# A hybrid decoder step on one Trainium2 core: the order of the attention's work on TensorE, wider key products, cache pages read earlier, four loop iterations written out

## The chip, the cores and the metric

The kernel runs on one NeuronCore of a Trainium2 chip. The metric is device time in microseconds (us) of one execution. Three runs of the kernel before took 1240.34, 1240.37 and 1240.64 us, with a median of 1240.37. The profiler's picture of one more execution (1240.44 us) gives the rows below.

## The reference

One inference step of a two-layer trunk with D = 1024, for 256 prompt tokens of one sequence and 64 sample tokens (8 sequences of 8). Layer 0 is half-FFN, mLSTM, half-FFN. Then one shared pair of keys and values is projected. Layer 1 is half-FFN, attention with 8 heads of 128, half-FFN, and a final RMSNorm. All is f32. Cut to the attention that the change touches:

```
# prompt: causal inside 256 tokens;  sample: 256 cached keys in 2 pages of 128, and 8 new ones
k_past = cache_k[page_table]          # pages of (128 keys, 8 heads, 128)
s = q @ k.T * 128**-0.5 - slope[head] * distance      # masked where distance < 0
out = softmax(s) @ v                  # per head, then @ w_out_b and x = x + out
```

With 256 keys and a block of 256 every query attends to all earlier keys.

## The kernel before

The 256 + 64 = 320 tokens are the moving columns of nearly every product; the weights are stationary, in tiles of 128 x 128. Weights come by DMA in units of 1 MB (or 0.7 MB) into a ring `raw` of four slots. ScalarE writes the upper part of each unit (`w_hi`), VectorE the lower part (`w_lo`), and TensorE adds three products in PSUM (`passes`, L556 to L558). A `pair_unit` is 16 such triples (two output chunks, 48 matmuls); an `out_chunk` of an FFN is 22 triples (66 matmuls). An FFN is 22 pair units and 8 output chunks. Most of them run in hardware loops: nine iterations of two pair units, three iterations of two output chunks. The third FFN (`f == 2`) is the one ahead of the attention; between them stand the four units of the query projection.

Each engine has an instruction list of its own, written out by hand, and semaphores order the lists. A change of one list does not move the others except through these waits. For the attention the lists are as follows.

**TensorE.** For prompt head h, `prompt_scores(h)` multiplies queries by keys (L954, L955). `prompt_turn(h)` transposes the probabilities with three transposes (L965). `prompt_outputs(h)` multiplies them by the values (L975, L976). For the sample tokens, 4 heads of 32 rows are packed into one PSUM bank. A product for one head then uses a 32-column strip of the array, and four strips work side by side. `new_scores` (L984) takes the new keys, and `cache_scores(b)` (L1001, L1007) the cached keys of sequence b. `turn_new_probs` and `turn_page_probs` (L1018, L1024) transpose, `new_outputs` (L1037) takes the new values and `cache_outputs(b)` (L1059) the cached ones. A *cached unit* c is the keys of sequence c for c < 8 and the values of sequence c - 8 otherwise. The order before puts these units into six visits, with prompt work between: units 0 and 1; 2 to 4; 5 to 7; 8 to 11; 12 to 14; 15. `turn_early_outputs` and `turn_late_outputs` (L1070, L1081) transpose the sample outputs. Then the output projection `w_ob` starts; its first product waits for the lower parts of head 0 and of the first late sample rows.

**Cache pages.** Cached units 0 to 3 and 9 to 12 use slots of the ring `raw`; the other eight use `rooms`, buffers that are otherwise idle at that time. In the ring the two pages of keys are one operand of 256 moving columns per head (L1007, 8 products a unit). In a room each page is multiplied by itself, 128 columns (L1001, 16 products a unit).

**SP (SyncE)** issues all weight and cache loads in one list. `page_of` (L493) reads a page number into a register with `value_load` and directly after it the DMA is issued (L504 in the ring, L509 in rooms). Each load waits for its slot (`slot_free`). Units 7 and up wait for the last unit of the query projection.

**ScalarE and VectorE.** ScalarE has `prompt_exp`, `prompt_copy` (transposed probabilities out of PSUM, L1545), `prompt_hi` (L1549), `sample_exp`, `sample_rows` and `late_hi` (L1568). VectorE has `prompt_bias` with the maxima (L2122, L2127), `prompt_probs` (L2134), `prompt_lo` (L2140), `sample_bias` (L2147), `spread_probs` (L2157, L2161) and `late_lo` (L2177). The prompt probabilities `pp` have two buffers, so the bias of head h waits for the transpose of head h - 2. All transposes of prompt probabilities use bank 6, one after the other. GpSimd clears `q_spread`, `p_spread` and `p_new` ahead of the attention.

Of the kernel before, what the change touches and what calls it, by code (L numbers as in the profile page):

```python
# [19 lines left out]
KT = D // 128  # L20
# [49 lines left out]
def trunk_program(nc, w_in, w_out, w_a, w_oa, w_kv, w_q, w_ob, w_gate, xp_in, con_in, row_in,  # L70
# [6 lines left out]
    with ctx:  # L77
# [30 lines left out]
        pp = work[:, 0:768].rearrange("p (s k) -> p s k", s=2)  # L108
        pt = work[:, 768:1536].rearrange("p (s k) -> p s k", s=2)
# [14 lines left out]
        with ExitStack() as ov:  # L124
# [35 lines left out]
            with ExitStack() as own:  # L160
# [9 lines left out]
                st = sb("st", [128, 2, 6], f32, own)  # L170
                sst = sb("sst", [128, 3, 4], f32, own)

        rooms = [[page_k[:, 0:1024], page_k[:, 1024:2048]], [keys_room[:, 0:1024], keys_room[:, 1024:2048]],
                      [row_room[:, 0:1024], norm_room[:, 0:1024]]]
        for at in (PAIR, 3 * PAIR):
            rooms.append([split_room[:, at:at + 1024], split_room[:, at + 1024:at + 2048]])
# [220 lines left out]
        def prompt_score_bank(h):  # L397

            return bank[{1: 6, H - 1: 1}.get(h, 5)]
# [31 lines left out]
        def _(sp):  # L431
# [60 lines left out]
            sp.wait_ge(s_pg, 16)  # L492
            def page_of(c, j):  # L493

                at = NPG * (c % NB) + j
                page = sp.value_load(pages[0:1, at:at + 1], min_val=0, max_val=kc_in.shape[0] - 1)
                return (kc_in if c < NB else vc_in)[bass.ds(page, 1), :, :].rearrange("a p c -> p (a c)")
# [55 lines left out]
        def _(pe):  # L553
# [103 lines left out]
            def ffn(f, h_wait, between, behind=None, values=0):  # L657
# [289 lines left out]

            def prompt_scores(h):
                if 2 <= h < H - 1:
                    pe.wait_ge(pr_b, h if h > 2 else 1)  # L950
                elif h == H - 1:
                    pe.wait_ge(sm_tc, 9)
# [5 lines left out]
            def prompt_turn(h):  # L958
# [5 lines left out]
                for i in range(3):  # L964
                    mm = pe.transpose(bank[6][:, i * 128:i * 128 + 128],  # L965
                                      pp[:, h % 2, i * 128:i * 128 + 128], ident)
# [20 lines left out]
            def cache_scores(b, groups=(0, 1)):  # L987
# [7 lines left out]
                for g in groups:  # L995
                    out = bank[2 * g + b // 4]
                    if early is not None:
# [6 lines left out]
                    else:  # L1004
                        keys = raw[:, raw_of_cache(b) % RAW, :].rearrange("p (j h k) -> p j h k", j=NPG, h=H)
# [7 lines left out]
            def turn_new_probs(i):  # L1013
# [3 lines left out]
                w = SLOT * (r % 2) + SLOT  # L1017
                pe.transpose(bank[r][0:w, 256:384], ss[:, r, PAST + SLOT - w:PAST + SLOT], ident)  # L1018
# [12 lines left out]
            def new_outputs(q):  # L1031

                outs = outs_of(q)
                pe.wait_ge(sm_tc, 6 * q + 6)
                for h in range(H):
# [48 lines left out]
            pe.wait_ge(x_ready, 4 * KT)  # L1084
            prompt_scores(0)
            prompt_scores(1)
            new_scores(0)
# [7 lines left out]
            cache_scores(0, (1,))  # L1095

            def cache_unit(c):

                if c < NB:
                    cache_scores(c)  # L1100
                else:
                    cache_outputs(c - NB)

            cache_unit(1)

            prompt_scores(2)
            prompt_turn(0)
            cache_unit(2)
            cache_unit(3)
            pe.wait_ge(qa_sp, 4)  # L1110
            cache_unit(4)

            prompt_outputs(0)
            prompt_scores(3)
            prompt_turn(1)
            cache_unit(5)
            cache_unit(6)
            cache_unit(7)

            turn_new_probs(0)  # L1120
            turn_page_probs(0)
            prompt_scores(4)
# [1339 lines left out]
```

## Time and profile before

| what | value |
|---|---|
| median of three runs | 1240.37 us |
| the profiled execution | 1240.44 us |
| its span in the trace | 1238.6 us |
| TensorE busy (matmuls; weight loads) | 1233.2 us; 1210.4 us |
| VectorE, ScalarE, GpSimd busy | 726.1; 582.7; 81.1 us |
| attention stage, 936.80 to 969.08 | 32.28 us |
| moved by DMA | 200.39 MB |

Busy time of an engine is the union of its records. A matmul's record lasts longer than the distance to the next one (309 ns each for the 320-column products, which follow one another about every 147 ns), because matmuls are pipelined and their ends are modelled. So a TensorE that is shown busy all the time can still pause; pauses are read from the distance between starts. PE is TensorE's matmuls, PEld its weight loads, DVE is VectorE, ACT is ScalarE, POOL is GpSimd. The largest groups of the page are all L556 to L558.

### The profile page before, as it was taken

What the parts mean: (1) busy time and instruction counts of PE and PEld (TensorE: products, weight loads), DVE (VectorE), ACT (ScalarE), POOL (GpSimd) and SP (SyncE); (2) the same over time, 40 slices, a digit from 0 to 9 for tenths busy, and PEclk for the clock granted to TensorE, in tenths of its full rate; (3) what the DMA queues carried; (4) which work ended last, traced back from release to release, by engine and by line L of the source; (5) the groups of instructions that cost most, each with busy time, mean ns of one, the idle gap of its engine ahead of it and who ended that gap; (6) DMA issues with size and microseconds to landing.
All of it is one profiled execution on the core that took longest, in us unless ns stands there. A gap on an engine that the chain in (4) does not pass through costs nothing.

```text
span 1238.6 us, 22056 instructions
## 1 busy us (share of the span) xinstructions
PE 1233.2 (100%) x8875; PEld 1210.4 (98%) x8875; DVE 726.1 (59%) x1127; ACT 582.7 (47%) x936; POOL 81.1 (7%) x99
## 2 busy tenths in 40 slices
PE   9999999999999999999999999999999999999998
PEld 9999999989999999999998999999998999999998
DVE  7656554575777656555564565655467585565443
ACT  6534333464556445443345554534344474544343
POOL 0000000100332000000000000000020110000010
PEclk9999999999999999999999999999999999999999
DMA  8344334543354443334543734334478734433341
GB/s 341 137 161 144 112 132 155 205 147 131 127 164 147 157 166 137 134 121 140 187 166 137 262 136 151 143 105 153 163 277 317 287 139 142 163 135 127 125 156 43
DMA packets 34778, 200.39 MB, mean 162 GB/s; under 512 B 4050, under 2 KB 4186, under 8 KB 19490
## 3 DMA queue, kind: packets, MB, share of 16 engines
q1 hardware_dynamic: 32706, 192.24, 44.0%
q0 software_dynamic: 2016, 7.39, 1.9%
q8 instruction: 38, 0.62, 0.2%
q14 instruction: 18, 0.15, 0.0%
HBM read 193.03 MB, written 6.57 MB: 161 GB/s over the span
## 4 chain that ended last, share of the span: by engine, by line
PE 99%; DMA 0%; SPq 0%; DVE 0%; ACT 0%; issue 0%; DVEq 0%
PE bank L556 30%; PE bank L558 30%; PE bank L557 29%; PE bank L714 1%; PE bank L713 1%; PE bank L712 1%; PE bank L716 1%; PE bank L715 1%; PE bank L1059 1%; DMA xp<-xp_in 0%; PE bank L867 0%; PE bank L822 0%; PE bank L975 0%; PE bank L1001 0%; PE bank L1007 0%; PE bank L955 0%
## 5 line engine op out<-in xcount | busy, mean ns | idle before, releaser
L556 PE MATMUL bank<-h_hi,w_hi 128*128 128x320 f32 x1792 | 555.6, 310 | 0.5 <-DVE h_lo L1682 0.5
L558 PE MATMUL bank<-h_hi,w_lo 128*128 128x320 f32 x1792 | 553.8, 309 | 0.0
L557 PE MATMUL bank<-h_lo,w_hi 128*128 128x320 f32 x1792 | 553.7, 309 | 0.0
L1222 ACT ACTIVATE w_hi<-raw 128x1024 fp32r<-128x1024 f32 (+1 forms) x364 | 331.7, 958 | 440.7 <-PE bank L558 421.7
L1668 DVE TENSOR_TENSOR w_lo<-raw,w_hi 128x1024 fp32r<-128x1024 f32 (+1 forms) x364 | 388.5, 1108 | 133.1 <-ACT w_hi L1222 133.0
L556 PEld LDWEIGHTS bank<-h_hi,w_hi 128*128 128x128 f32 x1792 | 336.3, 188 | 2.6 <-issue 1.4
L557 PEld LDWEIGHTS bank<-h_lo,w_hi 128*128 128x128 f32 x1792 | 336.4, 188 | 0.1
L558 PEld LDWEIGHTS bank<-h_hi,w_lo 128*128 128x128 f32 x1792 | 336.3, 188 | 0.0
L557 PE MATMUL bank<-f_lo,w_hi 128*128 128x320 f32 x704 | 216.5, 308 | 0.0
L558 PE MATMUL bank<-f_hi,w_lo 128*128 128x320 f32 x704 | 216.5, 308 | 0.0
L556 PE MATMUL bank<-f_hi,w_hi 128*128 128x320 f32 x704 | 216.5, 308 | 0.0
L1711 DVE TENSOR_TENSOR work<-bank,rms 128x320 f32<-128x320 f32 x88 | 43.2, 491 | 152.0 <-PE bank L558 151.5
L558 PEld LDWEIGHTS bank<-f_hi,w_lo 128*128 128x128 f32 x704 | 131.9, 187 | 0.0
L556 PEld LDWEIGHTS bank<-f_hi,w_hi 128*128 128x128 f32 x704 | 131.9, 187 | 0.0
L557 PEld LDWEIGHTS bank<-f_lo,w_hi 128*128 128x128 f32 x704 | 131.9, 187 | 0.0
L1272 ACT ACTIVATE f_hi<-work 128x320 f32 (+1 forms) x88 | 41.5, 472 | 124.0 <-DVE work L1719 124.0
L1726 DVE TENSOR_TENSOR f_lo<-work,f_hi 128x320 f32 (+1 forms) x88 | 43.3, 492 | 64.5 <-ACT f_hi L1272 64.5
L2281 POOL TENSOR_TENSOR norm_room<-norm_room 128x320 f32<-128x320 f32 x41 | 43.8, 1068 | 264.9 <-ACT norm_room L1244 263.7
L1731 DVE SCALAR_TENSOR_TENSOR xp<-bank,xp 128x320 f32<-128x320 f32 x31 | 15.3, 493 | 67.3 <-PE bank L558 67.3
L2278 POOL COPY norm_room<-norm_room 128x320 f32<-128x320 f32 x6 | 5.0, 836 | 723.1 <-ACT norm_room L1244 723.1
L1682 DVE SCALAR_TENSOR_TENSOR h_lo<-xp,h_hi 128x320 fp32r<-128x320 f32 x56 | 44.8, 833 | 3.4 <-ACT h_hi L1247 3.4
L1719 DVE TENSOR_TENSOR work<-work 128x320 f32<-128x320 f32 x88 | 42.8, 486 | 4.8 <-ACT work L1268 4.8
(263 smaller groups left out, 763.0 us busy)
## 6 DMA issues: line engine op xcount, KB each, us to landing
raw<-w_in SPq DMA_DIRECT2D x86, 1024.0 KB, 4.8
raw<-w_out SPq DMA_DIRECT2D x64, 704.0 KB, 4.0
raw<-w_a SPq DMA_DIRECT2D x12, 1024.0 KB, 4.7
raw<-w_kv SPq DMA_DIRECT2D x8, 1024.0 KB, 4.7
raw<-w_oa SPq DMA_DIRECT2D x4, 1024.0 KB, 6.0
raw<-w_q SPq DMA_DIRECT2D x4, 1024.0 KB, 4.7
raw<-w_ob SPq DMA_DIRECT2D x4, 1024.0 KB, 11.8
raw<-kc_in SPq DMA_DIRECT2D x8, 512.0 KB, 4.5
```

Source lines behind the costliest of these rows:

```text
L556: pe.matmul(out, wh, mh, start=first, stop=False)
L557: pe.matmul(out, wh, ml, start=False, stop=False)
L558: return pe.matmul(out, wl, mh, start=False, stop=last)
L1222: sc.activation(w_hi[:, n_at % 2, part * w:part * w + w], raw[:, raw_of(n_at) % RAW, part * w:part * w + w], ACT.Copy).then_inc(hi_done, 1)
L1272: sc.activation(dst, up[:, k_at % 2, :], ACT.Copy).then_inc(hid_hi, 1)
L1668: ins = ve.tensor_tensor(w_lo[:, n_at % 2, c], raw[:, raw_of(n_at) % RAW, c], w_hi[:, n_at % 2, c].bitcast(f32), ALU.subtract)
L1682: ve.scalar_tensor_tensor(out=h_lo[:, m, :], in0=x[:, m, :], scalar=par[:, P_G + KT * norm + m:P_G + KT * norm + m + 1], in1=h_hi[:, m, :] ...
L1711: ve.tensor_tensor(gate[:, k_at % 2, :], bank[b][:, 0:T], rms[:, :], ALU.mult).then_inc(gate_ready, 1)
L1719: ve.tensor_tensor(up[:, k_at % 2, :], up[:, k_at % 2, :], act[:, k_at % 2, :], ALU.mult).then_inc(hid_ready, 1)
L1726: ve.tensor_tensor(lo, up[:, k_at % 2, :], hi.bitcast(f32), ALU.subtract).then_inc(hid_lo, 1)
L1731: ve.scalar_tensor_tensor(out=x[:, m, :], in0=bank[4 + m % 2][:, 0:T], scalar=0.5, in1=x[:, m, :], op0=ALU.mult, op1=ALU.add).then_inc(x_r ...
L2281: gp.tensor_tensor(sqsum[:, :], sqsum[:, :], sq[:, m % 2, :], ALU.add).then_inc(sum_done, 1)
```

## The change

It does five things. (1) TensorE's list in the attention is in a new order: prompt scores of heads 0, 1 and 2 first, then cached units in four visits (0 to 6; 7 to 11; 12 to 14; 15). ScalarE's and VectorE's lists follow. Prompt scores of heads 2 and 4 go to bank 4, and `pp` and `st` have three buffers. (2) Rooms that are contiguous are used with 256-column key products as in the ring (cached units 4, 5 and 7; unit 6 lies in two tensors and stays as it was). (3) `turn_new_probs` transposes 128 columns of a widened `ss`, whose tail GpSimd clears. (4) SP reads the page numbers of units 7 to 13 ahead, between earlier loads. (5) In the third FFN the last two iterations of both loops are written out on TensorE.

```
-        pp = work[:, 0:768].rearrange("p (s k) -> p s k", s=2)
+        pp = work[:, 0:1152].rearrange("p (s k) -> p s k", s=3)
-                ss = sb("ss", [128, 4, PAST + SLOT], f32, own)
+                ss = sb("ss", [128, 4, PAST + 128], f32, own)
+        rooms = [[both[:, 0:1024], both[:, 1024:2048], both]
+                 for both in (page_k, keys_room, split_room[:, PAIR:2 * PAIR], split_room[:, 3 * PAIR:4 * PAIR])]
+        rooms.insert(2, [row_room[:, 0:1024], norm_room[:, 0:1024], None])
-            return bank[{1: 6, H - 1: 1}.get(h, 5)]
+            return bank[{1: 6, 2: 4, 4: 4, H - 1: 1}.get(h, 5)]
...
+            def read_pages(units):
+                for c in units:
+                    for j in range(NPG):
+                        at = NPG * (c % NB) + j
+                        page_read[c, j] = sp.value_load(pages[0:1, at:at + 1], min_val=0,
+                                                        max_val=kc_in.shape[0] - 1)
...
             load_room(6, 1)
+            read_pages((7,))
             load_cache(1)
+            read_pages((NB, NB + 1, NB + 2))
             load_cache(2)
+            read_pages((NB + 3, NB + 4, NB + 5))
             load_cache(3)
...
-                with pe.Fori(0, (FK - 4) // 2) as i:
+                looped = (FK - 4) // 2 - (2 if f == 2 else 0)
+                with pe.Fori(0, looped) as i:
-                pair_unit(u + FK - 1, p + FK - 1, u + FK - 1, p + FK - 1)
+                units(u, p, 3 + 2 * looped, FK)
...
-                with pe.Fori(0, (KT - 2) // 2) as i:
+                out_looped = (KT - 2) // 2 - (2 if f == 2 else 0)
+                with pe.Fori(0, out_looped) as i:
                     for j in (2, 3):
                         out_chunk(i * 2 + j, j, False)
+                for m in range(2 + 2 * out_looped, KT):
+                    out_chunk(m, m, False)
...
-                w = SLOT * (r % 2) + SLOT
-                pe.transpose(bank[r][0:w, 256:384], ss[:, r, PAST + SLOT - w:PAST + SLOT], ident)
+                at = PAST - SLOT * (r % 2)
+                pe.transpose(bank[r][:, 256:384], ss[:, r, at:at + 128], ident)
...
+            gp.memset(ss[:, :, PAST + SLOT:PAST + 128], 0.0).then_inc(spread_set, 1)
```

TensorE's list after the change, from the first prompt scores to the output projection (waits left out; S = prompt_scores, T = prompt_turn, O = prompt_outputs, n and p = turn_new_probs and turn_page_probs, N = new_outputs, bracketed numbers = cached units):

```
before: S0 S1 new_scores [0 1] S2 T0 [2 3 4] O0 S3 T1 [5 6 7] n0 p0 S4 T2 O1 n1 n2 S5 p1 p2 O2 T3
        N0 [8 9 10 11] n3 p3 O3 T4 S6 S7 T5 O4 N1 [12 13 14] T6 O5 early [15] T7 O6 late0 O7 late1
after:  S0 S1 S2 new_scores [0 1 2 3 4 5 6] T0 S3 n0 p0 T1 O0 S4 n1 T2 S5 p1 O1 [7] N0 [8 9 10 11]
        T3 O2 n2 S6 p2 T4 n3 O3 early p3 S7 T5 O4 N1 [12 13 14] O5 T6 [15] T7 O6 late0 late1 O7
```

## Rows read from the trace of the kernel before

**Rows 1.** The page: the span, and the chain of waits by engine.
```profile
span 1238.6 us, 22056 instructions
...
PE 99%; DMA 0%; SPq 0%; DVE 0%; ACT 0%; issue 0%; DVEq 0%
```

**Rows 2.** Stage table: stretch, length, busy time (records), clock, DMA share, GB/s.
```profile
936.80:969.08 32.28, 32.28 (x618) 26.84 (x617) 24.98 (x85) 16.99 (x59) 0.00 (x0) 1.00 1.00 380
...
970.00:1229.90 259.90, 259.90 (x1774) 259.90 (x1773) 140.93 (x197) 121.23 (x171) 18.28 (x15) 1.00 0.39 136
```

**Rows 3.** TensorE's timeline, entering two visits: start, length to the last end, operation, count.
```profile
937.68 0.60 PE L955 MATMUL bank<-k_all,qa 128*128 128x256 f32 x2
938.20 0.33 PE L984 MATMUL bank<-k_all,qa 128*32 128x32 f32 x16
...
961.38 0.65 PE L1037 MATMUL bank<-v_tok,p_new 128*32 128x128 f32 x16
961.84 1.06 PE L1059 MATMUL bank<-raw,p_spread 128*32 128x128 f32 x32
962.72 1.06 PE L1059 MATMUL bank<-page_k,p_spread 128*32 128x128 f32 x32
```

**Rows 4.** TensorE's timeline, the second visit, and what follows the fifth.
```profile
941.19 0.55 PE L965 MATMUL bank<-con,work 128*128 128x128 f32 x3
941.67 1.93 PE L1007 MATMUL bank<-raw,q_spread 128*32 128x256 f32 x32
943.42 1.06 PE L1001 MATMUL bank<-page_k,q_spread 128*32 128x128 f32 x32
944.41 0.70 PE L975 MATMUL bank<-work,v_tok 128*128 128x256 f32 x2
944.94 0.39 PE L976 MATMUL bank<-work,v_tok 128*128 128x128 f32 x2
...
964.58 0.55 PE L965 MATMUL bank<-con,work 128*128 128x128 f32 x3
964.96 0.60 PE L975 MATMUL bank<-work,v_tok 128*128 128x256 f32 x2
```

**Rows 5.** TensorE's timeline around the narrow transposes of new probabilities.
```profile
948.01 1.06 PE L1001 MATMUL bank<-split_room,q_spread 128*32 128x128 f32 x32
949.00 0.28 PE L1018 MATMUL bank<-con,ss 128*32 128x128 f32 x1
...
950.98 0.38 PE L1018 MATMUL bank<-con,ss 128*32 128x128 f32 x2
951.32 0.49 PE L954 MATMUL bank<-k_all,qa 128*128 128x128 f32 x2
```

**Rows 6.** SP's timeline: page issues of cached units 1 to 3, then unit 7.
```profile
921.65 14.00 SPq L504 DMA_DIRECT2D raw<-kc_in  x6
937.71 1.44 SPq L509 DMA_DIRECT2D split_room<-kc_in  x2
```

**Rows 7.** All engines' timeline at the end of the attention.
```profile
967.52 0.49 ACT L1545 ACTIVATE work<-bank 128x384 f32<-128x384 f32 x1 [0.52 <-PE bank L965]
...
968.02 0.27 PE L1081 MATMUL bank<-con,o_rows 128*128 128x128 f32 x1
...
968.33 0.28 ACT L1568 ACTIVATE h_hi<-bank 128x128 fp32r<-128x128 f32 x1 [0.32 <-PE bank L1081]
...
968.64 0.29 DVE L2177 TENSOR_TENSOR h_lo<-bank,h_hi 128x128 fp32r<-128x128 f32 x1 [0.90 <-ACT h_hi L1568]
...
969.08 0.38 PE L556 MATMUL bank<-h_hi,w_hi 128*128 128x320 f32 x1
```

**Rows 8.** DMA of 936.80 to 969.08, instruction queue: packets, MB, share of 16 engines.
```profile
q8 instruction: 5, 0.08, 1.0%
```

**Rows 9.** DMA issues of 934 to 936 and 942 to 950.5, median us to landing.
```profile
raw<-kc_in SPq DMA_DIRECT2D x2, 512.0 KB, 4.6
...
raw<-vc_in SPq DMA_DIRECT2D x8, 512.0 KB, 7.1
```

More of the change, by code:

```diff
@@ L166, in trunk_program @@
                 p_new = sb("p_new", [128, 4, 128], f32, own)
-                ss = sb("ss", [128, 4, PAST + SLOT], f32, own)
+                ss = sb("ss", [128, 4, PAST + 128], f32, own)
                 o_rows = sb("o_rows", [128, 4, DV], f32, own)
                 page_k = sb("page_k", [128, 2048], f32, own)
-                st = sb("st", [128, 2, 6], f32, own)
+                st = sb("st", [128, 3, 6], f32, own)
                 sst = sb("sst", [128, 3, 4], f32, own)
[L173 to L176, printed above, removed]
+        rooms = [[both[:, 0:1024], both[:, 1024:2048], both]
+                 for both in (page_k, keys_room, split_room[:, PAIR:2 * PAIR], split_room[:, 3 * PAIR:4 * PAIR])]
+        rooms.insert(2, [row_room[:, 0:1024], norm_room[:, 0:1024], None])
         ident, ones = con[:, C_ID:C_ID + 128], ones_r[:, :].bitcast(f32)
@@ L492, in _ @@
             sp.wait_ge(s_pg, 16)
+            page_read = {}
+            def read_pages(units):
[4 more added lines that the diff above has]
+                                                        max_val=kc_in.shape[0] - 1)
             def page_of(c, j):
-                at = NPG * (c % NB) + j
-                page = sp.value_load(pages[0:1, at:at + 1], min_val=0, max_val=kc_in.shape[0] - 1)
-                return (kc_in if c < NB else vc_in)[bass.ds(page, 1), :, :].rearrange("a p c -> p (a c)")
+                if (c, j) not in page_read:
+                    read_pages((c,))
+                return (kc_in if c < NB else vc_in)[bass.ds(page_read[c, j], 1), :, :].rearrange("a p c -> p (a c)")
             def load_cache(c):
@@ L996, in cache_scores @@
                     out = bank[2 * g + b // 4]
-                    if early is not None:
+                    if early is not None and rooms[early][2] is None:
                         for j in range(NPG):
@@ L1004, in cache_scores @@
                     else:
-                        keys = raw[:, raw_of_cache(b) % RAW, :].rearrange("p (j h k) -> p j h k", j=NPG, h=H)
+                        both = raw[:, raw_of_cache(b) % RAW, :] if early is None else rooms[early][2]
+                        keys = both.rearrange("p (j h k) -> p j h k", j=NPG, h=H)
                         for k in range(QB):
@@ L1084, in _, with cache_unit @@
             pe.wait_ge(x_ready, 4 * KT)
+            def cache_unit(c):
+                if c < NB:
+                    cache_scores(c)
+                else:
+                    cache_outputs(c - NB)
             prompt_scores(0)
             prompt_scores(1)
+            prompt_scores(2)
             new_scores(0)
@@ L1095, in _ @@
             cache_scores(0, (1,))
[L1097 to L1106, printed above, removed]
-            prompt_turn(0)
[L1108 to L1113, printed above, removed]
+            for c in range(1, 4):
+                cache_unit(c)
+            pe.wait_ge(qa_sp, 4)
+            for c in range(4, 7):
+                cache_unit(c)
+            prompt_turn(0)
             prompt_scores(3)
[L1115 to L1118, printed above, removed]
             turn_new_probs(0)
             turn_page_probs(0)
+            prompt_turn(1)
+            prompt_outputs(0)
             prompt_scores(4)
+            turn_new_probs(1)
             prompt_turn(2)
-            prompt_outputs(1)
-            turn_new_probs(1)
-            turn_new_probs(2)
             prompt_scores(5)
             turn_page_probs(1)
-            turn_page_probs(2)
-            prompt_outputs(2)
-            prompt_turn(3)
+            prompt_outputs(1)
+            cache_unit(7)
             new_outputs(0)
@@ L2119, in prompt_bias @@
                 ve.wait_ge(pr_s, h + 1)
-                if h >= 2:
-                    ve.wait_ge(pr_t, h - 1)
-                ve.scalar_tensor_tensor(out=pp[:, h % 2, :], in0=con[:, C_ND:C_ND + 384], scalar=SLOPE[h],
+                if h >= 3:
+                    ve.wait_ge(pr_t, h - 2)
+                ve.scalar_tensor_tensor(out=pp[:, h % 3, :], in0=con[:, C_ND:C_ND + 384], scalar=SLOPE[h],
                                         in1=prompt_score_bank(h)[:, 0:384], op0=ALU.mult, op1=ALU.add
```

104 lines of the change are left out of this document (55 added, 49 removed).

## The prediction

> **What bounds the kernel now.** I read the page first, then the stage table, then the timeline of the one stage that the change touches. The page says that TensorE is busy in all of the 1238.6 us and that the chain of waits lies on it for 99% [rows 1]. So time comes off only where TensorE does less, or where the starts of its instructions lie further apart than their columns ask. The stage table puts the attention at 936.80 to 969.08, 32.28 us, 618 matmul records, at the full granted clock (1.00, the 2.4 GHz level); the long stretch behind it, 970 to 1229.9, has the same clock and a full busy share [rows 2]. That busy share hides pauses, since ends are modelled. The timeline shows them: I subtract start from start.
>
> The unit of account is one pass (an f32 product is two passes and two records, a transpose one). A cached unit of 128-column products is 32 records in eight slots of four passes side by side, 961.84 to 962.72: 0.109 us a slot [rows 3]. Two units with 256-wide keys are 32 records from 941.67 to 943.42, less 0.02 of entry (below) 1.73 us in eight slots: 0.216 us [rows 4]. All that is more is pause.
>
> **Where the pauses are.** Entering a visit of cached products (four 32-column tiles side by side) from whole-array work: 937.68 to 938.20 is 0.52 against 2 x 0.216, so 0.09; then 961.38 to 961.84 is 0.46 against 4 x 0.109, so 0.02. Together 0.12 us with the thousandths [rows 3]. Leaving: the unit from 943.42 takes 0.99 against 0.875, so 0.11 before the next product, and that product's two 256-column passes take 0.53 against 0.43, so 0.10 more: 0.22 into a product. Into three transposes: from 962.72 [rows 3] to 964.58 lie two units of 0.875, which leaves the same 0.11 of 1.86, and 964.58 to 964.96 is 0.38 against 0.33: 0.17 in all [rows 4]. Into a narrow transpose (32 columns stationary): 948.01 to 949.00 gives 0.12, and I take 0.13; the two narrow ones at 950.98 take 0.34 against 0.22 before a product begins, and with the product's own second pause that is 0.22 once more [rows 5].
>
> **The change part by part.**
> 1. *Visits.* Before there are six: out of them the exits cost 0.22, 0.22, 0.13, 0.14, 0.17 and 0.17, the narrow pair 0.22, and six entries 6 x 0.12 = 0.72. Sum 1.99 us. After there are four, and what follows them is a transpose (heads 0, 3 and 7) or a product (outputs of head 5): 4 x 0.12 + 3 x 0.17 + 0.22 = 1.21. The transposes of new probabilities now have 128 stationary columns and need no switch. Gain 0.78.
> 2. *The wait of the first prompt transpose.* At 941.19 it starts 0.11 late, held by the first probabilities, and its three passes and the entry behind them show the loads uncovered: 0.48 to 941.67 against 0.33 + 0.09, so 0.06 [rows 4]. After, it stands behind seven cached units, 945.3 instead of 941.2, and the probabilities are ready at about 941. Gain 0.17. What is late next is in 6.
> 3. *256-wide keys in rooms.* Units 4, 5 and 7 go from 16 products to 8. A narrow unit is 8 x 0.109 = 0.875, a wide one 4 x 0.216 = 0.865: gain 0.01 each, 0.03 [rows 3, 4].
> The page TensorEngine Tiling (Array Packing) of the Trainium skill, section Instruction Overhead, speaks of some 60 cycles for each matmul; by it 24 products fewer would give 24 x 25 ns = 0.6 us. The trace disagrees (0.875 against 0.865 us), and the sum goes by the trace.
> 4. *Three prompt scores ahead.* The same products in another place; they need only bank 4, whose last reader is done when x is ready. Price 0. Cover: none needed, TensorE does them anyway.
> 5. *Pages read ahead, on SP.* A page goes out every 1.10 us with its read (two issues in 1.44 us, the last 0.34), the issue alone being 0.34, so a read is at most 0.76 us and six are at most 4.6 [rows 6]. I take 0.57, half of the 1.10 and a little, 3.4 us for six. Read between cached loads 1 and 2 and between 2 and 3, they fall into waits for a free slot: the six issues of loads 1 to 3 take 14.00 us for work of 6 x 1.1, so some 3.7 us of wait stand ahead of each of 2 and 3. Load 3's second page still goes out at 935.3, at the bound 4.6 up to 1 us later, and B below has room for 1.7. Behind it the queue gets shorter: units 7 to 12 go out in about 0.55 instead of 1.10 us a page, so the values and the output weights come earlier than before. Gain on TensorE 0, bounds: 0 (nothing waits for a transfer now) and -0.8 (a late page, below). The extra memset of 384 columns on POOL ends near 920, and its wait on VectorE stands at 933. Price 0.
> 6. *Waits of the new order.* I carried each engine's list along with its durations: copy of transposed probabilities 0.49, upper part 0.28 and lower part 0.29 us for late sample rows [rows 7], 0.1 more for a whole head, and on VectorE, start to next start, bias with maxima 1.11 and probabilities 0.66. The tightest places on TensorE, by how long before need the word comes: transpose 1 behind copy 0, 0.1 us; outputs 2 behind lower part 1, 0.1; outputs 3 and 4, 0.2 each; transpose 7, 0.25; the second new outputs behind the last spread probabilities, 0.3. Behind a waiting instruction here everything on TensorE waits. Bounds: 0 (all covered) and 0.3 us (several missed by 0.05 to 0.1, each with its 0.06 to 0.10 of uncovered load). I take 0.
> 7. *The end.* The first product of the output weights waits for the lower part of the late sample rows. Before: transpose at 968.02, upper part 968.33, lower part 968.64, product 969.08, that is 1.06 us from transpose to product [rows 7]. That chain stays, and in both orders the last outputs (0.65) and the other late transpose (0.11) stand behind this transpose and fit into the 1.06. So TensorE stands some 0.3 us here after as before, and what counts is what lies ahead of 968.02: 0.78 + 0.17 + 0.03 = 0.98 us, and the transpose comes at 967.04. Bounds: 0, and 0.1 gained by short waits ahead of the last outputs that I cannot tell from the rounding.
> 8. *Four loop iterations written out.* The loop bodies are the same products. Branches show no cost: 970 to 1229.9 holds nine and three iterations of these loops, and TensorE and its loads are both busy 259.90 of 259.90 us [rows 2]. What the edit adds is code: 4 x 96 + 4 x 132 = 912 records in straight line. In the attention 1235 records took five instruction loads, one per 247, so it adds 3.7 loads, and each takes 1.0% x 16 x 32.28 / 5 = 1.03 us of a DMA engine [rows 8]. With a load per some 18 us of such stages (247 records, matmuls 0.147 us apart with a weight load each) the load is far ahead. Value 0; bounds -1.03 us (one load uncovered) and 0 (no iteration boundary costs anything that could come back).
> The page Advanced Engine Details and Errata of the Trainium skill, section ISA Cache, says that instructions come in lines of 256; by that rule, the trace agrees (247), and straight code has to be fetched where a loop had not.
>
> **The sum.** Of the profiled execution: 1238.6 - 0.98 = 1237.6 us span; with the 1.84 around it, 1240.44 - 0.98 = 1239.46. It stands 0.07 above the median 1240.37, and from that the same sum gives 1239.4, which I predict.
>
> **The rivals.**
> A. *Instruction supply (the slower side).* The new order packs seven cached units in a row and shifts by 912 records where each load falls. Where 128-column products run, 64 records (with their weight loads) pass in 0.875 us and 247 in 3.4 us, against 1.03 us for a load while the DMA share is 1.00 [rows 2]. One load uncovered gives 1239.4 + 1.03 = 1240.4; from the second on the kernel is slower, 1241.4. It decides when the loads are late by more than 0.98 us in total. For it: more straight code, full rings. Against: five loads in the same stage now, without a pause that the switches do not explain.
> B. *A page is late.* Cached unit 3 is wanted at 941.7 instead of 942.5. It lands at 935.3 + 4.6 = 939.9 [rows 9]; if the four page loads that now follow faster stretch it to the 7.1 us of the value pages [rows 9], it lands at 942.4, 0.7 to 0.8 late: 1240.2.
> C. *The vector and scalar engines are late.* The margins of 6 are missed: 0.3 us, 1239.7.
> D. *The pauses are not those of the switch*, but come with the first product of any group that changes operands; then fewer visits bring nothing and only the removed wait counts: 1240.2. Against: prompt scores followed by prompt scores, and transposes by products, run without a pause.
> E. *A fixed cost per product*, which fewer products save: 24 of them at the 0.02 that the first slot of a visit costs [rows 3] give 0.5 more, 1238.9. Against: the 0.875 and 0.865 of part 3.
>
> **How the numbers follow.** Forecast 0.69, A 0.10 (0.06 of it one load), B 0.05, C 0.08, D 0.04, E 0.04. Within 0.2% (2.5 us; about what can be told from no change) lie all of these but several uncovered loads: same 0.93. Slower by more needs 3.5 us of them, 0.04; faster by more has no term, 0.03. The range 1238.8 to 1240.6 holds the forecast, B to E, and one load of A.
>
> **What would show it.** The first product of the output weights at 968.1. Four entries of 0.09 and none at the transposes of new probabilities. First prompt transpose at 945.3 with no wait for VectorE. Cached unit 3 without a pause. No gap over 0.1 us in the rest of the third FFN, above all where the loops end. I am wrong if TensorE stands for an instruction load or a page, or if exits cost less or more in the new neighbourhood.

## The result, and the profile after

| kernel | median | runs, lowest to highest |
|---|---|---|
| before, same chip | 1240.24 us | 16, 1239.94 to 1240.64 |
| changed | 1243.30 us | 16, 1241.60 to 1244.09 |

The ratio is 1.0021 with a 95% interval of 1.0014 to 1.0028: slower, and outside the range forecast. The medians differ by 3.1 us; the ratio alone would give 2.6, since the runs are split as follows. The changed kernel's runs fall into two groups: six of 1241.6 to 1242.1 us have a granted clock of 1.000, ten of 1243.2 to 1244.1 us one of 0.998 or 0.999. The profiled execution, 1243.27 us, is of the second.

The page of the changed kernel, the lines that answer to [rows 1]: the span is 2.9 us longer and the chain is still TensorE's.
```profile
span 1241.5 us, 21936 instructions
...
PE 99%; DMA 0%; issue 0%; SPq 0%; DVE 0%; ACT 0%; DVEq 0%
```

Its stage table (columns as in [rows 2]): the attention, then a stretch within it.
```profile
936.67:972.42 35.75, 33.27 (x570) 27.61 (x569) 25.04 (x86) 17.88 (x61) 0.00 (x0) 0.95 0.99 398
957.28:960.80 3.52, 3.52 (x37) 2.94 (x29) 0.00 (x0) 0.86 (x2) 0.00 (x0) 0.52 1.03 410
```
The attention is 35.75 us long instead of 32.28, 3.47 more. TensorE, busy throughout before, now has 35.75 - 33.27 = 2.48 us without a record, and for 3.5 us its clock is half (0.52).

Where this lies is in its timeline (start, length to the last end, operation, count, in brackets the idle time ahead and what ended it):
```profile
944.84 0.40 PE L1019 MATMUL bank<-norm_room,q_spread 128*32 128x128 f32 x8
945.17 0.55 PE L983 MATMUL bank<-con,work 128*128 128x128 f32 x3
...
949.93 0.38 PE L994 MATMUL bank<-work,v_tok 128*128 128x128 f32 x2
950.24 1.07 PE L1026 MATMUL bank<-split_room,q_spread 128*32 128x256 f32 x16
951.13 0.62 PE L1058 MATMUL bank<-v_tok,p_new 128*32 128x128 f32 x16
951.57 1.06 PE L1080 MATMUL bank<-split_room,p_spread 128*32 128x128 f32 x32
952.44 1.48 PE L1080 MATMUL bank<-raw,p_spread 128*32 128x128 f32 x44
956.38 2.33 PE L1080 MATMUL bank<-raw,p_spread 128*32 128x128 f32 x52 [2.46 <-issue]
958.64 0.90 PE L983 MATMUL bank<-con,work 128*128 128x128 f32 x3
959.34 1.06 PE L993 MATMUL bank<-work,v_tok 128*128 128x256 f32 x2
960.19 0.64 PE L994 MATMUL bank<-work,v_tok 128*128 128x128 f32 x2
```
TensorE stops in the middle of cached unit 10, between two products of one line that wait for nothing ("issue"). I call such a stop a stand. By starts the gap is 953.65 to 956.38: 2.63 us over the slot of 0.109. From 0.9 to 1.0 us after the restart a slot takes 0.213 us instead of 0.109, until 960.8: the last row but one, the two passes of a 256-column product, takes 0.85 instead of 0.43. This stretch costs some 3.52 x (1 - 0.52) = 1.7 us. So 2.63 + 1.7 were added, and the rest is 3.47 - 4.33 = -0.86: the saving. The medians of the two groups of runs lie 1243.4 - 1241.8 = 1.6 us apart, about the half-clock stretch. So I read the groups as the stand in all runs and the lower clock behind it in ten; only one execution has a trace.

What is missing is the supply of instructions. Rows of four answers of the DMA view: the kernel before from its border (explained below) to 953.1 and from there 0.1 us on, then the changed kernel likewise. q1 carries pages and weights, q8 instructions; the share is that of the time of 16 DMA engines:
```profile
q1 hardware_dynamic: 297, 1.08, 103.4%
...
q8 instruction: 1, 0.02, 69.3%
```
```profile
q1 hardware_dynamic: 718, 2.61, 102.0%
...
q8 instruction: 1, 0.02, 67.2%
```
The first row of each covers 950.54 to 953.10 in the kernel before and 947.41 to 953.75 in the changed one, and no instruction packet is among its packets; the second covers 953.10 to 953.20 and 953.75 to 953.85, and the packet starts there. A load brings 256 instructions (one packet of 0.02 MB; the changed kernel has 41 loads for its 10571 instructions, the kernel before 38 for 9750). I counted TensorE's instructions in the program, weight load and matmul one each. All the stands below lie at a number that is 215 or 216 modulo 256, here 8408: I call such a place a border. In the kernel before, the load needed at the border of 956.5 us starts 2.6 us behind the border ahead of it; here it starts 6.4 us behind (953.79, border 947.41), when TensorE has already started its last product ahead of the stand (953.65). In every kernel with a stand TensorE goes on 2.2 to 2.6 us after such a late load's start, though its packet takes 0.9 to 1.1: here 956.38 - 953.79 = 2.59.

The other rows of the forecast came out. Entries of 0.09 and 0.02, four of them. An exit into transposes of 0.11 and then 0.06: the two slots from 944.84 end at 945.06, and the first transpose starts at 945.17. No pause at the transposes of new probabilities. The first prompt transpose at 945.17 without a wait. SP's issues, with the landing times of the value pages:
```profile
937.00 0.85 SPq L518 DMA_DIRECT2D split_room<-kc_in  x2
938.03 0.85 SPq L518 DMA_DIRECT2D split_room<-vc_in  x2
940.25 5.63 SPq L513 DMA_DIRECT2D raw<-vc_in  x8
```
```profile
raw<-vc_in SPq DMA_DIRECT2D x8, 512.0 KB, 9.4
```
Two issues take 0.85 where they took 1.44 [rows 6]; the values land after 9.4 instead of 7.1 us [rows 9], and nothing waits for them here.

### The profile page after: what moved, and what is told of

It is laid out like the page before. It is cut to its first block, busy times and chain, and to the rows that moved or that the text cites. A ratio compares the mean times of both kernels' runs of the same rounds, so it can differ in the third digit from the quotient of the medians.

```text
span 1241.5 us, 21936 instructions
## 1 busy us (share of the span) xinstructions
PE 1233.8 (99%) x8827; PEld 1210.7 (98%) x8827; DVE 726.2 (58%) x1127; ACT 583.3 (47%) x936; POOL 81.4 (7%) x100
## 4 chain that ended last, share of the span: by engine, by line
PE 99%; DMA 0%; issue 0%; SPq 0%; DVE 0%; ACT 0%; DVEq 0%
PE bank L568 30%; PE bank L570 29%; PE bank L569 29%; PE bank L730 1%; PE bank L729 1%; PE bank L728 1%; PE bank L1080 1%; PE bank L732 1%; PE bank L731 1%; PE bank L1026 0%; DMA xp<-xp_in 0%; PE bank L883 0%; PE bank L838 0%; PE bank L993 0%; PE bank L973 0%; PE bank L983 0%
```

## The experiments

Each job ran the kernel before on the same chip: 1240.57 us in the first job, 1240.28 in the second, 1240.39 in the third, 1240.24 in the fourth. "Order" is the new order with three-deep buffers.

### First job: the parts one by one

`e1_reads_on_demand`, the page reads back at their loads (both of a unit together):
```
-            read_pages((7,))
-            read_pages((NB, NB + 1, NB + 2))
-            read_pages((NB + 3, NB + 4, NB + 5))
```


> The changed kernel, but SP reads each page number right before its DMA as before the change. In the changed kernel TensorE stood from 953.65 to 956.38 us in the middle of a cached unit, with no semaphore there, and an instruction load started at that moment. Theory Q (queue): the pages issued 0.52 us apart instead of 1.10 us fill the DMA rings (value pages landed after 9.4 to 13.6 us instead of 7.1), and the instruction load that TensorE needs waits behind them; then here the load comes in time, no stand, 1239.4 us. Theory P (place): the new order and the written-out iterations put the border between two instruction loads into a run that TensorE works off too fast for any load; then the stand of 2 to 3 us stays, 1242 to 1243.5 us.

1242.06 us (1240.73 to 1243.81), ratio 1.0014 [1.0005, 1.0023]. The stand is there, 2.9 us at the same instruction 8408. The reads ahead are not its cause. The clock of this profiled execution stays full behind it.

`e2_loops_kept`, the loops as they were:
```
-                looped = (FK - 4) // 2 - (2 if f == 2 else 0)
+                looped = (FK - 4) // 2
-                out_looped = (KT - 2) // 2 - (2 if f == 2 else 0)
+                out_looped = (KT - 2) // 2
```


> The changed kernel with all loop iterations of the third FFN in the loops again; page reads stay ahead. All borders between instruction loads move by 912 records (156 within a load of 256). Theory Q: the rings are as full as in the changed kernel, but the distance between borders around the visit of units 8 to 11 grows from 6.2 to 8.2 us (943.98 to 952.22 by the records of the changed kernel), so the stand shrinks to 0 to 1 us: 1239.4 to 1240.5 us. Theory P: the dense run still holds a border, so a stand of 2 to 3 us stays, elsewhere: 1242 to 1243.5 us.

1242.35 us (1241.18 to 1243.93), ratio 1.0013 [1.0004, 1.0022]. The stand at 8408 is gone and another is there, 2.2 us at instruction 7896, border again, with half clock behind it; and TensorE waits 0.7 us for the page of unit 11 (0.9 by starts). Taking the written-out iterations away moves the loss and does not remove it.

`e3_before_written_out`, the kernel before with part 8 alone, and `e4_before_reads_ahead`, with part 5 alone:

> The kernel before with only the four loop iterations written out. Theory Q: page loads go out as slowly as before, instruction loads are some 3 us late and need 2.6 us more to be usable, and the borders lie 7.7, 7.3, 5.1 and 5.4 us apart, so at most a stand of 0.6 us near 959.4: 1240.2 to 1241. Theory P: writing out is what puts a border into a dense run, so a stand of 2 to 3 us with the half clock behind it: 1242 to 1244 us. If nothing of both: 1240.2.

> The kernel before with only the page numbers read ahead on SP. Theory Q: the rings fill as in the changed kernel, an instruction load is 5 to 6 us late plus 2.6, and the borders lie 5.7 to 6.8 us apart, so TensorE stands 1 to 3 us: 1241.5 to 1244 us. Theory P: borders are where they were, no stand, 1240.2 us.

e3: 1240.79 us, ratio 1.0002 [0.9993, 1.0011], a stand of 0.5 us at a border (8919). e4: 1240.29 us, 0.9997 [0.9988, 1.0006], attention 32.28 us, no stand, though its value pages land after 9.6 us as in the changed kernel. Neither part alone costs what was lost: for e3 theory Q's time holds, for e4 theory P's.

### Second job: place and traffic

`e5_order_and_width`: both edits of e1 and e2 together, so that only the order and the wide keys are left.

> The changed kernel with its page reads back beside their loads and its loops kept: only the order of the visits and the width of the keys are left of the change. TensorE's program is the one of the run with the loops kept, so its borders of 256 instructions (at 216 modulo 256) stand at the same places. Theory P (place: a load of 256 instructions comes too late where TensorE gets through the 256 before it too fast): the stand in the last value visit, at about 964.5 us, stays, 1.5 to 2.5 us, and the time is 1241.2 to 1243 us. Theory O (the order itself costs, by late pages or waits of vector and scalar work, and the instructions are a side effect): a time of 1241 to 1243 us too, but with a wait for a semaphore of over 0.5 us in the attention. If neither: no stand, 1239.4 us, and the written-out iterations would be the whole loss.

1242.83 us (1241.34 to 1245.60), ratio 1.0021 [1.0012, 1.0030]. A stand of 1.93 us at 7896 and, as the theory O had it, a wait for a page:
```profile
PE bank L1077 <- issue: 1.8, 1, 1.8
PE bank L1077 <- DMA raw<-vc_in: 1.2, 1, 1.2
```
So the order, with the wide keys, brings a loss of this size without the other parts, in two kinds: where no instruction stand delays TensorE ahead of unit 11, that unit's page is late. The order also moves which products lie between two borders, so this run doesn't tell the two apart.

`f1_one_pair_iteration` (the changed kernel) and `f2_before_one_pair_iteration` (the kernel before) move the borders by writing out one iteration of the pair loop and none of the other:
```
-                looped = (FK - 4) // 2 - (2 if f == 2 else 0)
+                looped = (FK - 4) // 2 - (1 if f == 2 else 0)
-                out_looped = (KT - 2) // 2 - (2 if f == 2 else 0)
+                out_looped = (KT - 2) // 2 - (0 if f == 2 else 0)
```


> The changed kernel with one loop iteration of the fused pairs written out instead of two and two: TensorE's attention begins at instruction 7050 instead of 7772, so its borders fall 78, 334, 590, 846 and 1102 products and weight loads behind its start instead of 124, 380, 636, 892 and 1148. Nothing else differs. Theory P: the stretches between borders then take 5.6, 8.1, 8.1 and 4.6 us without a stand (7.3, 6.6, 8.1, 5.6 in the changed kernel), so no stand in units 8 to 11, at most one of under 1 us at the last border (about 966 us): 1239.3 to 1240.5 us. Theory R (the instruction load is held up by the full DMA rings, wherever the border is): a stand of 2 us or more somewhere between 948 and 958 us, 1242 to 1243.5 us. Theory S (the spare length of the program, more loads in all, is what costs): between, in proportion to 39 loads instead of 41, about 1241.

> The kernel before with one loop iteration of the fused pairs written out, nothing else. Its attention then begins at instruction 7050 and its borders fall 78, 334, 590, 846 and 1102 behind that; between the third and the fourth TensorE needs only 3.5 us (5.5 us in the kernel before, whose shortest this is beside 6). Theory P: a stand of 1.5 to 2 us at about 957.5 us (846 instructions into the attention), with or without a stretch at half clock behind it of up to 1.7 us: 1241.7 to 1243.9 us, in the order of before. Theory R: the pages are issued 1.1 us apart as in the kernel before, the rings hold 2 MB at most, so no stand: 1240.3 us.

f1: 1242.17 us (1241.42 to 1242.82), ratio 1.0015 [1.0006, 1.0024], stands of 1.73 and 0.86 us and one of 0.3 us at 945.13, all at borders. Theory P had none at the place of the 1.73; it fails as stated, since the load there starts 7.4 us behind its border. Theory R's time fits (1242 to 1243.5), its stand of 2 us or more does not.

f2: 1244.58 us (1244.18 to 1245.93), ratio 1.0035 [1.0023, 1.0047], the slowest of all, with the order, the widths and the page issues of the kernel before. Its stage table row and the rows at the first stand:
```profile
936.88:974.34 37.46, 34.62 (x619) 28.38 (x617) 24.98 (x85) 17.11 (x59) 0.00 (x0) 0.95 0.98 378
```
```profile
955.00 2.78 PE L1063 MATMUL bank<-raw,p_spread 128*32 128x128 f32 x90
959.80 0.42 PE L1063 MATMUL bank<-raw,p_spread 128*32 128x128 f32 x6 [2.01 <-issue]
...
960.51 1.06 PE L979 MATMUL bank<-work,v_tok 128*128 128x256 f32 x2
```
The stand (2.17 us, at 957.51) comes where P put it, a second of 1.0 us follows at 968.1, and the last row shows the half clock (0.86 us for the two passes of a 256-column product). The time is 0.7 us above P's upper bound; P had one stand. One written-out iteration, in a stretch of 320-column products that itself takes no longer (the attention begins at 936.88 instead of 936.80), costs 4.3 us some 130 us later: the last branch of its loop is at 807.4 us, one iteration takes 14.1. This shows that the kernel before is free of stands only by where its borders fall.

`f3_small_value_pages` leaves out 15/16 of the cached values from the second value unit on, in the changed kernel:
```
+                n = 1024 if c <= NB else 64
-                    sp.dma_start(raw[:, r % RAW, j * 1024:j * 1024 + 1024], page_of(c, j)
+                    sp.dma_start(raw[:, r % RAW, j * 1024:j * 1024 + n], page_of(c, j)[:, 0:n]
```


> The changed kernel with 64 instead of 1024 columns of each cached value page read from the second value unit on (so 15/16 of those values are left out, and what the room held is used in their place); all instructions and waits of TensorE are as in the changed kernel. Theory R: with the rings nearly empty between 941 and 953 us the instruction load starts within 3 us of TensorE's crossing of the border at 947.4 us, the stand at 953.6 us is gone, 1239.3 to 1239.8 us. Theory P in its strict form (the load takes the same time whatever the rings hold): the stand of 2.6 us stays at the same instruction, 1241.6 to 1243.3 us.

1239.26 us (1239.01 to 1239.71), ratio 0.9992 [0.9983, 1.0001]. Of the stand 0.17 us is left.
```profile
936.77:968.44 31.67, 31.65 (x570) 26.29 (x569) 25.04 (x86) 17.95 (x61) 0.00 (x0) 1.00 0.68 239
```
TensorE's program is the same to the instruction, so traffic has a part in it: the load starts at 951.41, 2.4 us earlier. But the load still starts 3.9 us behind its border, with these rows from the border (947.51) to 951.38, and from there 0.1 us on:
```profile
q1 hardware_dynamic: 432, 0.10, 11.3%
...
q8 instruction: 1, 0.02, 70.4%
```
What the expectations call rings, the DMA queues by q1's share, is all but empty (11.3%) while it has not started, so traffic is not all that holds it.

### Third job: controls

`g1_before_small_value_pages`: the same cut in the kernel before.

> The kernel before with 64 instead of 1024 columns of each cached value page read from the second value unit on (15/16 of those values left out). A control for the changed kernel with the same cut, which took 1239.26 us. Theory G (that run shows the 0.98 us that the visits and the turns save, with the stand gone): there is no stand in the kernel before that could go, so 1240.2 us, attention 32.2 to 32.3 us long, and the two differ by 0.9 to 1.0 us. Theory H (emptier rings by themselves give the time back): 1239.3 us here too.

1240.31 us (1240.13 to 1240.68), ratio 0.9999 [0.9990, 1.0008].
```profile
936.74:969.02 32.28, 32.28 (x619) 26.84 (x617) 24.97 (x85) 16.99 (x59) 0.00 (x0) 1.00 0.63 219
```
Theory G holds. Against f3 the medians differ by 1.05 us. In the attention 0.60 us of it is seen, 0.77 without f3's 0.17 of stand, where the sum had 0.98; in the profiled executions 0.35 us more lies behind TensorE's last product, in no term of the sum.

This run says something of the loads too. With the pages full, those that follow the borders of 950.54 and 956.5 us start 2.6 and 3.0 us behind them (953.12 and 959.52). Here they start at 950.27, 0.3 us ahead, and at 956.80, 0.3 us behind, in the same program of TensorE. So the traffic holds a load back by some 3 us.

`g2_one_pair_small_pages`: the cut in f2.

> The kernel before with one pair iteration written out (1244.6 us, stands of 2.17 and 1.01 us and half clock behind them) and with 64 instead of 1024 columns of the later value pages. TensorE needs 3.6 us between the borders at 590 and 846 instructions of its attention. Theory P (place alone): both stands stay, 1243 to 1244.6 us. Theory PR (place and rings together: the load starts later after the crossing where the rings are full): a load that starts 1.5 to 3.9 us behind the crossing and is usable 2.5 us later leaves a stand of 0.4 to 2 us at the first and none at the second: 1240.8 to 1242.5 us.

1241.99 us (1241.47 to 1244.34), ratio 1.0016 [1.0007, 1.0025], against f2's 1244.58. The first stand is gone and one of 1.67 us appears at the second place, where the load starts 6.0 us behind its border. The time fits place and rings together, the places of the stands do not.

`g3_reads_one_by_one` gives the changed kernel the page reads of the kernel before, each at its load, and `g4_one_by_one_one_pair` does so in f1; the pages then go out 1.1 us apart.

> The changed kernel with the page numbers read one by one, each beside its load, as in the kernel before, so that two loads of 512 KB are issued 1.1 us apart and never 0.5 us. Order, width, written-out iterations and TensorE's program stay. Theory PR: with the rings as shallow as in the kernel before, the load asked for at the border of 947.5 us starts 2.6 to 3.9 us later as there, and the stand at 953.7 us is gone or under 0.3 us: 1239.3 to 1239.8 us. Theory PO (the order itself makes the load late, whatever the pages' pace): a stand of 2.5 to 3 us at the same instruction, 1241.5 to 1243.3 us, as with the reads in pairs.

> The same with one pair iteration written out in place of two and two, so that the borders fall 78, 334, 590, 846 and 1102 instructions behind the start of the attention (stands of 1.73 and 0.86 us with the pages read ahead, 1242.2 us). Theory PR: no stand at 953.7 us, at most 0.9 us at the last border, where 4.6 us lie between the borders: 1239.4 to 1240.4 us. Theory PO: stands of 1.7 and 0.9 us as with the reads ahead, 1241.4 to 1242.5 us.

g3: 1243.26 us (1240.41 to 1243.72), ratio 1.0020 [1.0011, 1.0029], a stand of 2.633 us where the changed kernel has 2.632. g4: 1241.65 us, ratio 1.0010 [1.0001, 1.0019], 1.728 and 0.861 where f1 has 1.727 and 0.858. My theory that bursts of pages delay the load falls flat. Stands equal to some ns under different page issues suggest that the request goes out at a fixed point of TensorE's own course. They do not show it: e1, the same program of TensorE with yet other page issues, has a stand of 2.91 us.

### Fourth job: a wait between two borders

That point was open. TensorE's sequencer, the part that reads the instructions and holds them at a wait, leaves a record at some waits (PEldq). The one for `pr_lo` ahead of the second head's outputs (L992) stands 9 instructions ahead of instruction 8192 (32 x 256), in the changed kernel. The expectations call 8192 the border, though the border by the stands is 8152, 31 instructions ahead of this wait; that 8192 has a meaning of its own no run shows. The wait and the VectorE row that releases it:
```profile
L992 PEldq EVENT_SEMAPHORE  x1: 51/51/51, 948.6 to 948.6; - x1
...
948.20 0.39 DVE L2159 TENSOR_TENSOR h_lo<-bank,h_hi 128x256 fp32r<-128x256 f32 x1
```
VectorE is done at 948.59 and the sequencer goes on at 948.63, so it was held, though TensorE, still working on what was queued, shows no pause: the product behind the wait starts at 949.5.

`h1_late_wait` makes it end later, `h2_late_wait_small_pages` does so in f3, and `h3_early_wait` takes the wait to behind instruction 8192 (the second part of the diff; VectorE's list first, then TensorE's and ScalarE's):
```
             spread_probs(0)
-            prompt_lo(0)
             prompt_bias(4)
+            prompt_lo(0)
...
-            prompt_outputs(1)
             cache_unit(7)
+            prompt_outputs(1)
             ...
-            prompt_hi(1)
             prompt_copy(2)
             sample_exp(2)
+            prompt_hi(1)
```


> The changed kernel with two steps of VectorE exchanged: the lower halves of the first prompt head's outputs come behind the bias of the fifth head's scores instead of ahead of it, so that the wait 9 instructions ahead of TensorE's instruction 8192 ends at about 949.7 us instead of 948.6 us. Theory HS (held sequencer): TensorE itself loses 0.3 us there, the load starts 1.0 to 1.2 us later (at about 954.9 us) and the stand grows from 2.63 to 3.2 to 3.6 us; 0.8 to 1.3 us over the changed kernel's 1243.3 us. Theory P (place and traffic alone): the stand stays 2.6 us within 0.1, and the time grows by 0.3 us at most.

> The same exchange in the kernel with 64 instead of 1024 columns of the later value pages (1239.26 us, a stand of 0.17 us at instruction 8408, the load started at 951.41 us). Theory HS: load at about 952.5 us, stand of 0.8 to 1.1 us, 1240.0 to 1240.6 us. Theory P: no more than 0.3 us of a wait of its own, 1239.3 to 1239.6 us.

> The changed kernel with the outputs of the second prompt head, and so the wait for the lower halves, moved from ahead of the eighth key unit to behind it (and ScalarE's steps reordered to suit), so that the wait stands behind instruction 8192. One more entry and exit of a visit cost TensorE 0.3 to 0.4 us. The last wait ahead of the border then ends at about 947.6 us. Theory HS: the load starts at about 952.8 to 953.2 us, and the stand at instruction 8408 falls from 2.63 to 1.3 to 1.9 us: in all 0.4 to 1.0 us under the changed kernel. Theory P: the stand stays at 2.4 to 2.7 us, and the time rises by the 0.3 to 0.4 us of the visit.

h1: 1243.96 us (1242.60 to 1244.35), ratio 1.0025 [1.0014, 1.0036]. TensorE itself now waits:
```profile
950.25 0.67 PE L993 MATMUL bank<-work,v_tok 128*128 128x256 f32 x2 [0.40 <-DVE h_lo L2159]
...
957.49 2.34 PE L1080 MATMUL bank<-raw,p_spread 128*32 128x128 f32 x52 [2.74 <-issue]
```
Measured from the start of the attention the wait ends 1.3 us later and the load starts 1.1 us later (955.10), as expected; TensorE lost 0.6 us itself, not 0.3, so the stand grew only to 2.91 us. Load and stand moved though place and traffic did not: P fails, and HS is right on the load and high on the stand and on the time (0.7 us over the changed kernel where it had 0.8 to 1.3). Of the load's 1.1 us of delay 0.6 is as much as TensorE itself was delayed.

h2: 1239.58 us (1239.48 to 1240.19), ratio 0.9996 [0.9986, 1.0005]. The load starts 0.7 us later, measured from the start of the attention, and TensorE's own wait of 0.6 us eats that: no stand. The time is P's (1239.3 to 1239.6), HS's stand of 0.8 us is missing, and this run does not tell a held sequencer from a delayed TensorE.

h3: 1239.64 us (1239.39 to 1240.14), ratio 0.9995 [0.9985, 1.0005], 3.7 us under the changed kernel. The rows show the unit that had the stand, and the stage:
```profile
951.99 0.65 PE L1058 MATMUL bank<-v_tok,p_new 128*32 128x128 f32 x16
952.45 1.06 PE L1080 MATMUL bank<-split_room,p_spread 128*32 128x128 f32 x32
953.33 3.12 PE L1080 MATMUL bank<-raw,p_spread 128*32 128x128 f32 x96
956.38 0.55 PE L983 MATMUL bank<-con,work 128*128 128x128 f32 x3
```
```profile
937.23:969.16 31.93, 31.80 (x571) 26.03 (x569) 25.06 (x86) 17.89 (x61) 0.00 (x0) 1.00 1.01 398
```
96 passes run through where 44 and 52 stood apart; the only pause left is one of 0.3 us behind the product of 954.99. It stands ahead of the first product of unit 11, where e2 and e5 wait for the page, and the view of the weight loads puts it to that page too (0.4 us for `raw<-vc_in`). The traffic is that of the changed kernel (398 GB/s in both), the program has the same length, and the attention takes 31.93 us instead of 35.75. The load starts at 951.84: from the start of the attention 2.5 us earlier, where HS had 0.6 to 1.0 and a stand of 1.3 to 1.9 us left. So moving one group of products whose wait never cost TensorE a pause removes the stand. It is the order of products and of waits that was changed, and the run doesn't tell which of them the load follows. The attention fits the forecast's account: 32.28 - 0.98, and 0.3 for the page and 0.35 for one more entry and exit, give 31.95, so here the sum comes out whole. h3 stands 0.6 us under the kernel before, less than these runs can tell from no change; it is the best version found that computes everything.

## Why the prediction was wrong

1. *Visits* (0.78), *the wait of the first transpose* (0.17), *wide keys* (0.03): right in their mechanism, pause by pause, and somewhat too large in sum: 0.77 us in the attention between f3 and g1, 0.86 by the account of the changed kernel's own trace. Where the missing 0.1 to 0.2 lies I did not find. Rivals D and E are out: D had a saving of 0.17 us in all, E one of 1.5.
2. *Prompt scores ahead* and *pages read ahead* (0): right for the time. e4 is level with the kernel before. The later landing of the values costs nothing in the changed kernel. Rival B's place, unit 3, was never late; but a page was, unit 11's, by 0.3, 0.9 and 1.3 us between starts, in kernels without an instruction stand ahead of it (h3, e2, e5). I had looked for a late page only where loads were reordered, not where TensorE would reach a unit sooner.
3. *Waits of the new order* (0, bound 0.3): none was missed as idle time, C is out. But I priced a wait by the idle time of TensorE alone. The wait for the lower halves, whose margin was good enough for that, held the sequencer, and in h1 and h3, which move it, the instruction load moves too (1.1 us later, 2.5 us earlier). Whether the wait itself or the course of the products does it is not separated.
4. *The end* (1.06 of chain kept) is as forecast:
```profile
971.37 0.38 PE L1102 MATMUL bank<-con,o_rows 128*128 128x128 f32 x2
...
971.68 0.28 ACT L1588 ACTIVATE h_hi<-bank 128x128 fp32r<-128x128 f32 x1 [0.27 <-PE bank L1102]
...
971.99 0.29 DVE L2196 TENSOR_TENSOR h_lo<-bank,h_hi 128x128 fp32r<-128x128 f32 x1 [1.17 <-ACT h_hi L1588]
...
972.42 0.38 PE L568 MATMUL bank<-h_hi,w_hi 128*128 128x320 f32 x1
```
971.37 to 972.42 is 1.05 us, against the 1.06 of [rows 7].
5. *Loop iterations written out* (0, bound -1.03), and with it rival A, is the step that failed. The mechanism named there, an uncovered instruction load, is the one that came; place, condition and price were wrong. The price of one was taken from the time that a load's packet takes, 1.03 us [rows 8]. What the changed kernel paid is a stand of 2.63 us and, in ten of 16 runs, a stretch at half clock that costs 1.7 us. TensorE goes on not when a late load's packet ends but 2.2 to 2.6 us after it starts, and with full pages the packet starts 1.4 to 7.5 us after the border ahead of it is passed. Together that is 4 to 10 us, against some 6 to 7 us that TensorE takes from border to border in the attention before: there was no cover of the kind that I reckoned with (247 instructions in 3.4 us against a load of 1.0). Five loads in 32.28 us, one in 6.5, I had; the 2.2 to 2.6 us no row of the kernel before shows, since it has no stand. With them its load of 953.12 was in time for the border of 956.5 by only some 0.9 us. With the price at 2.6 to 4.3, one late load makes the kernel 1.6 to 3.3 us slower, so A's share of "one load uncovered" should have stood on the slower side.

What made it late is partly settled. The order with the wide keys does (e5), the written-out iterations move it to another border (e2, f1) and by themselves can bring it about in the old order (f2). Place (f2) and traffic (f3 against the changed kernel, g1 against the kernel before) are each shown to move it by changing nothing else of weight; for the wait this is only likely, as h1 also delays TensorE and h3 also moves products. Open is the rule that joins them: why h3's load came 2.5 us earlier when taking the wait away spares only 1.0 us of holding, why g2's stand went to the other border, and what decides whether the clock falls behind a stand.

## What to carry to other kernels

Straight-line code of short instructions has a second budget beside the engine's time: count the instructions between two borders of 256, look how long the engine needs for them, and compare that with the whole course of a load as the trace shows it (packet start to resumption, and border to packet start), not with the packet's duration. A kernel near that limit can gain or lose 4 us by code added 130 us earlier, so a change there is judged only together with a run that shifts the borders. And a wait that costs no idle time need not be free: h1 and h3 moved one and lost 0.7 and gained 3.7 us. Look at when the sequencer passes it, and try another place.

## What the runs showed of the hardware

- TensorE stood at instruction 215 or 216 modulo 256 of its program for 0.3 to 2.9 us, in eleven kernels (the changed one, e1, e2, e3, e5, f1, f2, g2, g3, g4, h1), with "issue" as the only reason given; it resumed 2.2 to 2.6 us after the load's packet (16 KB, 0.9 to 1.1 us) had started.
- With q1 at 102% of the DMA engines' time the packet started 6.4 us behind the border, with q1 at 11% 3.9 us, same program of TensorE (f3). In the kernel before and g1 two loads started 2.6 and 3.0 us behind their borders with full pages, 0.3 us ahead and 0.3 us behind with small ones.
- Behind stands of 1.9 to 2.9 us the granted clock was half for 3 to 4 us (0.52 in 957.28 to 960.80) in the profiled executions of the changed kernel, e2, e5, f2 and h1, beginning 0.4 to 1.0 us after the restart; ahead of it TensorE had idled for the length of the stand. In those of e1 (2.9 us) and g3 (2.6 us) it stayed full. The page TensorE: Matmul & The Clock Gate of the Trainium skill, section The HAM clock gate, says that the clock follows how busy the array has lately been and that the moment of a change differs from run to run; that ten of 16 runs of one kernel had the half clock and six had not fits that, though the page speaks of the moment and not of whether the change comes.
- Eight 256-column key products cost as much as 16 of 128 columns: 0.86 us for a wide unit in the changed kernel (942.46 to 943.32) against 0.875; beyond this 0.01 the 24 products fewer show no fixed cost.
